# Query projection in fp32r halves, rotated scores in two row halves of the array, the mask added by VectorE, and all cache pages issued by one queue

## What is computed

```python
cq = rms_norm(h @ w_dq)                               # N x 512
q = (cq @ w_uq).reshape(T, 8 heads, 128 + 64)         # 128 plain, 64 to be rotated
q_nope, q_rope = q[..., :128], rope(q[..., 128:], pos)
s = (q_lat . kv_lat + q_rope . kv_rope) * scale       # masked causally, softmax
o_lat = softmax(s) @ kv_lat;  y = (o_lat @ w_uv) @ w_o
```

## Time and profile before

| | |
|---|---|
| median of 3 runs | 3227.74 us |
| the profiled execution | 3235.13 us |
| its span (first to last instruction) | 3233.5 us |
| TensorE busy | 2474.1 us (77%) |
| VectorE busy | 1346.7 us (42%) |
| ScalarE busy | 1083.1 us (33%) |
| granted TensorE clock, mean | 0.866 |

### The profile page before, as it was taken

One profiled execution on the slowest core, in us unless ns is written; L12 is line 12 of the kernel. 1 busy time (PEld: TensorE's weight loads), 2 busy tenths in 40 slices (PEclk: granted clock), 3 DMA queues, 4 the chain that ended last, 5 costly groups with the idle time before them and its releaser, 6 DMA issues. The chain is left out here.

```text
span 3233.5 us, 39140 instructions
## 1 busy us (share of the span) xinstructions
PE 2474.1 (77%) x11571; PEld 1799.5 (56%) x11571; DVE 1346.7 (42%) x2113; ACT 1083.1 (33%) x1738; POOL 405.0 (13%) x492
## 2 busy tenths in 40 slices
PE   3999975858608999896788999997668438999960
PEld 1866654647507777775454666663257326777740
DVE  2311114546534644642771222231145526644647
ACT  1211212331114655653332333231122026655542
POOL 0000001520020010000321000002400020000005
PEclk6899985778759999998798999998778669999985
DMA  6166624630126756664314000006640038755754
GB/s 221 49 239 218 211 96 115 201 113 26 40 104 221 285 208 249 244 223 162 139 64 153 12 23 11 14 9 213 205 147 33 27 119 326 261 212 214 256 208 142
DMA packets 197663, 486.22 MB, mean 150 GB/s; under 512 B 23539, under 2 KB 59604, under 8 KB 191078
## 3 DMA queue, kind: packets, MB, share of 16 engines
q1 hardware_dynamic: 165366, 385.33, 34.3%
q0 software_dynamic: 25152, 74.12, 7.0%
q10 hardware_dynamic: 7056, 25.69, 1.9%
HBM read 423.89 MB, written 64.37 MB: 151 GB/s over the span
## 5 line engine op out<-in xcount | busy, mean ns | idle before, releaser
L1809 DVE TENSOR_TENSOR e_wl<-e_raw,e_wh 128x1024 fp32r<-128x1024 f32 x384 | 447.1, 1220 | 339.7 <-ACT e_wh L1757 332.5
L1757 ACT CAST e_wh<-e_raw 128x1024 fp32r<-128x1024 f32 x384 | 373.8, 1046 | 176.7 <-SPq L1664 74.4
L1716 PE MATMUL e_psG<-e_wh,e_xh 128*128 128x512 f32 x784 | 311.9, 398 | 30.8 <-DVE e_xl L1822 30.8
L1717 PE MATMUL e_psG<-e_wl,e_xh 128*128 128x512 f32 x784 | 311.4, 397 | 0.0
L1718 PE MATMUL e_psG<-e_wh,e_xl 128*128 128x512 f32 x784 | 311.2, 397 | 0.0
L1716 PE MATMUL e_psY<-e_wh,e_hh 128*128 128x512 f32 x392 | 168.2, 429 | 39.4 <-DVE e_hl L1831 39.4
L1716 PEld LDWEIGHTS e_psG<-e_wh,e_xh 128*128 128x128 f32 x784 | 148.2, 189 | 67.4 <-issue 31.6
L309 PE MATMUL in_ps<-in_w_upper,in_h_upper 128*128 128x512 f32 (+1 forms) x432 | 178.7, 414 | 0.0
L310 PE MATMUL in_ps<-in_w_lower,in_h_upper 128*128 128x512 f32 (+1 forms) x432 | 172.7, 400 | 0.0
L311 PE MATMUL in_ps<-in_w_upper,in_h_lower 128*128 128x512 f32 (+1 forms) x432 | 172.0, 398 | 0.0
L1717 PEld LDWEIGHTS e_psG<-e_wl,e_xh 128*128 128x128 f32 x784 | 148.2, 189 | 35.8
(11 more groups left out here) (435 smaller groups left out, 4384.0 us busy)
## 6 DMA issues: line engine op xcount, KB each, us to landing
e_raw<-in_e_gate SPq DMA_DIRECT2D x32, 2048.0 KB
e_raw<-in_e_up SPq DMA_DIRECT2D x32, 2048.0 KB
e_raw<-in_e_down SPq DMA_DIRECT2D x32, 2048.0 KB, 14.8
x<-in_ada_w SPq DMA_DIRECT2D x40, 1024.0 KB, 5.3
yrows<-e_y ACTq DMA_DIRECT2D x49, 512.0 KB, 7.2
x<-in_cache SPq DMA_DIRECT2D x80, 192.0 KB, 3.5
in_w_raw<-in_a_w_in POOLq DMA_DIRECT2D x48, 256.0 KB, 4.4
qkvo<-in_out SPq DMA_DIRECT2D x48, 256.0 KB, 2.3
```

Of the source, the lines that this page charges most:

```text
L1716: T.matmul(out, upper[:, k, :], wh[:, z, cols], start=first and i == 0, stop=False)
L1717: T.matmul(out, upper[:, k, :], wl[:, z, cols], start=False, stop=False)
L1757: S.copy(wh[:, z, c * PC:(c + 1) * PC], raw[:, z, c * PC:(c + 1) * PC]).then_inc(s_hi[z], 1)
L1809: V.tensor_tensor(wl[:, z, at], raw[:, z, at], wh[:, z, at].bitcast(F32), ALU.subtract).then_inc(s_lo[z], 1)
```

## The change

**Latents.** `cqT` is kept as an fp32r upper half `cqh` (ScalarE's copy in `back`) and an fp32r rest `cql`, which VectorE subtracts (`lower(t)`, one more 128 x 512 instruction per tile, after `normalise` of the next tile); TensorE waits for it before it reuses the PSUM tile. The weights `wkv` and `wdq` are placed where `mixT1` will be, which frees memory.

**Query projection.** The head's `wq` is split by ScalarE (`split(h)`, 128 x 1024, to fp32r) and VectorE (`lower(h)`, 128 x 1024). For head h+1 both stand in block i = 2 of head h's loop. TensorE makes three fp32r matmuls where one fp32 matmul stood, over runs of 364, 364 and 360 columns.

**Rotation.** VectorE's product goes to `prod`; ScalarE copies it with its two 64-partition halves swapped (`swap_halves`, two copies of 64 partitions), VectorE adds the two (`add_halves`) into `qr`, so both halves of `qr` hold the rotated query.

**Scores.** Block i above 0 is cut in two column halves w = 64(i+1), each in a PSUM bank of its own. The plain part is one fp32 matmul per half. The rotated part is one fp32 matmul per half with a contraction over 64 partitions, column half 0 on partitions 0 to 63 and half 1 on 64 to 127. The mask product is gone; VectorE adds the mask to the diagonal 128 x 128 in PSUM ahead of the maximum.

**Pages.** POOL issues none. In the heads stage SP issues the same 32 key pages and no values are loaded there. In the sample stage SP issues key units 4 to 15 and value units 0 to 15 (224 pages) in order of use; the values have four buffers. After the last head's projections SP loads head 0's weights once more, for the split that the loop's last pass makes.

The diff, cut to its core:

```diff
@@ stage_combine_latents
-                S.copy(g.cqT[:, :, t * P:t * P + n], psC[:, :, 0:n])
+                S.copy(g.cqh[:, :, t * P:t * P + n], psC[:, :, 0:n])
+            def lower(t):
+                v.wait_ge(s_out, t + 1)
+                V.tensor_tensor(g.cql[:, :, t * P:t * P + n], psC[:, :, 0:n],
+                                g.cqh[:, :, t * P:t * P + n].bitcast(F32), ALU.subtract).then_inc(s_cql, 1)
@@ stage_heads
-        RUNS = ((0, HALF), (HALF, HALF), (SEQ, NSAMP))
+        RUNS = ((0, 364), (364, 364), (728, 360))
-        @block.gpsimd
-            po.dma_start(pt[:], g.page_table).then_inc(s_pt, 16)
-            po.wait_ge(s_pt, 16)
-            for u in range(len(g.vals)):
-                load_unit(po, g, pt, u, g.vals[u], VALUE_COLS, g.s_vals[u])
+            sp.dma_start(pt[:], g.page_table).then_inc(s_pt, 16)
...
+            sp.wait_ge(s_job, JOBS * H + JOBS)
+            weights(0)
@@ tensor
                 pe.wait_ge(s_w, 64 * h + 64)
+                pe.wait_ge(s_wl, h + 1)
-                            mm = T.matmul(psJ[:, z, 0:n], wq[:, k, z * P:(z + 1) * P], g.cqT[:, k, lo:lo + n],
-                                          start=(k == 0), stop=(k == 3))
+                            T.matmul(out, wqh[:, k, cols], g.cqh[:, k, c], start=(k == 0), stop=False)
+                            T.matmul(out, wqh[:, k, cols], g.cql[:, k, c], start=False, stop=False)
+                            mm = T.matmul(out, wql[:, k, cols], g.cqh[:, k, c], start=False, stop=(k == 3))
...
-                        T.matmul(psS[:, par, lo:hi], qn[:, q], kT[:, lo:hi], start=True, stop=False)
-                        mm = T.matmul(psS[:, par, lo:hi], qr[:, q], g.krT[:, lo:hi], start=False, stop=not last)
-                            mm = T.matmul(psS[:, par, i * P:width], g.ident[:], g.qmask[:], start=False, stop=True)
+                    for a in range(parts):
+                        T.matmul(psS[:, par, a, 0:w], qn[:, q], kT[:, a * w:(a + 1) * w], start=True, stop=False)
+                    for a in range(parts):
+                        mm = T.matmul(psS[:, par, a, 0:w], qr[64 * a:64 * a + 64, q],
+                                      g.krT[64 * a:64 * a + 64, a * w:(a + 1) * w], start=False, stop=True)
@@ scalar
+            def split(h):
+                act.wait_ge(s_w, 64 * h + 64)
+                S.copy(wqh[:], wq[:]).then_inc(s_wh, 1)
+            split(0)
...
+                    for a in range(2):
+                        S.copy(swap[64 * a:64 * a + 64, r % 2, 0:n], prod[64 - 64 * a:128 - 64 * a, r % 2, 0:n])
...
                     if i >= 1:
                         output(i - 1)
+                    if i == 2:
+                        split(h + 1)
@@ vector
+            def lower(h):
+                v.wait_ge(s_wh, h + 1)
+                V.tensor_tensor(wql[:], wq[:], wqh[:].bitcast(F32), ALU.subtract).then_inc(s_wl, 1)
...
+                    own = psS[:, par, parts - 1, w - P:w]
+                    V.tensor_tensor(own, own, g.qmask[:], ALU.add)
+                    v.drain()
...
                     if i + 1 < PT:
                         maximum(i + 1)
+                    if i == 2:
+                        lower(h + 1)
@@ stage_sample
+            load_keys(4)
+            for u in range(RV):
+                load_values(u)
+            sp.dma_start(wv, g.w_uv.rearrange("h p n -> p h n")).then_inc(s_wv, 16)
+            for u in range(5, 10):
+                load_keys(u)
+            for u in range(10, UNITS):
+                load_keys(u)
+                load_values(u - 6)
+            for u in range(UNITS - 6, UNITS):
+                load_values(u)
         @block.gpsimd
-            for u in range(len(g.vals), UNITS):
-                if u >= RV:
-                    po.wait_ge(s_vu, u - RV + 1)
-                load_unit(po, g, pt, u, vals[u % RV], VALUE_COLS, s_vals[u % RV])
```

More of the change, by code:

```diff
@@ L2091, in turn_latents @@
                     pe.wait_ge(s_out, t)
+                    pe.wait_ge(s_cql, t)
                 for k in range(4):
@@ L2264, in _ @@
                 normalise(t)
+                if t >= 1:
+                    lower(t - 1)
+            lower(TILES - 1)
 def stage_heads(nc, g):
@@ L2293, in stage_heads @@
         block = ctx.enter_context(nc.Block())
-        RUNS = ((0, HALF), (HALF, HALF), (SEQ, NSAMP))
+        RUNS = ((0, 364), (364, 364), (728, 360))
+        WIDE = 364
+        SAMPLE = slice(SEQ - RUNS[2][0], N - RUNS[2][0])
+        prod, swap = sb("rope_products", [P, 2, WIDE]), sb("rope_swapped", [P, 2, WIDE])
+        s_wh, s_wl, s_swap, s_qr = (sem(x) for x in ("wq_upper", "wq_lower", "halves_swapped", "q_rope_ready"))
         JOBS = 11
         ACT_JOBS = 8 + PT
-        @block.gpsimd
-        def _(po):
-            po.dma_start(pt[:], g.page_table).then_inc(s_pt, 16)
-            po.wait_ge(s_pt, 16)
-            for u in range(len(g.vals)):
-                load_unit(po, g, pt, u, g.vals[u], VALUE_COLS, g.s_vals[u])
         @block.sync
@@ L2417, in _ @@
                     S.copy(qn[:, lo:lo + n], psJ[:, 0, 0:n]).then_inc(s_ja, 1)
+                    if r >= 1:
+                        swap_halves(r - 1)
                 for c in range(2):
@@ L2467, in _, with rotate, add_halves @@
             v.wait_ge(s_c, 16)
+            def lower(h):
+                v.wait_ge(s_wh, h + 1)
+                V.tensor_tensor(wql[:], wq[:], wqh[:].bitcast(F32), ALU.subtract).then_inc(s_wl, 1)
+            lower(0)
             with v.Fori(0, H) as h:
-                for r, (lo, n) in enumerate(RUNS):
+                def rotate(r):
+                    lo, n = RUNS[r]
                     v.wait_ge(s_job, JOBS * h + JOBS + 2 * r + 2)
-                    V.tensor_tensor(qr[:, lo:lo + n], psJ[:, 1, 0:n], trig[:, lo:lo + n], ALU.mult).then_inc(s_jv, 1)
+                    V.tensor_tensor(prod[:, r % 2, 0:n], psJ[:, 1, 0:n], trig[:, lo:lo + n], ALU.mult).then_inc(s_jv, 1)
+                def add_halves(r):
+                    lo, n = RUNS[r]
+                    v.wait_ge(s_swap, 3 * h + r + 1)
+                    V.tensor_tensor(qr[:, lo:lo + n], prod[:, r % 2, 0:n], swap[:, r % 2, 0:n], ALU.add).then_inc(s_qr, 1)
+                rotate(0)
+                rotate(1)
+                add_halves(0)
+                v.drain()
+                rotate(2)
+                add_halves(1)
+                add_halves(2)
                 def maximum(i):
@@ L2557, in _, with load_keys @@
             sp.wait_ge(s_pt, 16)
-            for u in range(len(g.keys), UNITS):
+            def load_keys(u):
                 if u >= RK:
@@ L2562, in _, with load_values @@
                 load_unit(sp, g, pt, u, keys[u % RK], KEY_COLS, s_keys[u % RK])
-                if u == len(g.keys):
-                    sp.dma_start(wv, g.w_uv.rearrange("h p n -> p h n")).then_inc(s_wv, 16)
+            def load_values(u):
+                if u >= RV:
+                    sp.wait_ge(s_vu, u - RV + 1)
+                load_unit(sp, g, pt, u, vals[u % RV], VALUE_COLS, s_vals[u % RV])
+            load_keys(4)
[9 more added lines that the diff above has]
+                load_values(u)
         @block.gpsimd
```

66 lines of the change are left out of this document (43 added, 23 removed).

## The result

The changed kernel takes **3341.58 us** (median; 3337.87 to 3344.08) against 3227.44 for the one before (3225.49 to 3228.67): a ratio of 1.0353, 95% interval 1.0335 to 1.0371. It is slower, by 114 us between the medians. The two profiled executions lie closer, 3235.13 before and 3337.87 after, 102.7 apart, and it is this difference that the traces can share out. I cut both at SP's first issue of a stage: 6.1 less up to the latents stage (code that the change leaves alone), 0.4 more in the latents stage, **3.5 more in the heads** (1718.54 to 2191.87 before, 1712.79 to 2189.66 after), **102.4 more in the sample stage** (to 2361.05 and 2461.19), 2.6 more behind it.

A forecast was written before the change was run, and what follows sets the result against it. It took page issue on the queues to bound the sample stage and TensorE the heads. Sample +104, heads -7, clock +8, once +5.5 made +110.5, rounded to +111: 3346 profiled, less 7.4 gives median 3339, range 3308 to 3364.

The forecast's parts named there:

- A page's time is the queue's: Page loads: the interval is the cost of issuing, above all the page-number read, whatever the size; 1.09 to 1.14 us.
- The rival that bytes set it: Sample stage: value pages cost two thirds, 0.75 us, so sample +57 and total 3292; chance 0.08.
- Sample stage +104: SP issues 224 pages at 1.12 us without stopping; last page issued at about 2446 instead of 2341.75.
- Issuing is nearly free: Sample stage rival: one queue gives bytes as fast as two, below 0.63 us a page; 3214, faster; chance 0.03.
- Projection -3.8 a head: Heads, query projection: three fp32r matmuls per former fp32 one take 11.9 us a head instead of 15.72.
- Row halves -3.75 and mode changes +3.4: Heads, rotated scores: 64-row halves run side by side, but two mode changes in each of 8 blocks cost 0.21 each.
- Mask -1.7, its waits +1.4: Heads: dropping eight 0.22 us mask products saves TensorE 1.7; VectorE's addition lengthens waits in four blocks by 1.4.
- The chain's 0.37: Heads: VectorE's mask addition ahead of the maximum, 0.29 us plus some 0.08 until the next instruction.
- Split and lower +3.6: Heads: VectorE's lower waits for ScalarE's split ahead of block 3's division, delaying TensorE 3.6 us a head.
- Clock +8: Heads: extra idling makes the other five heads lose 1.6 us each at lower clock; between nothing and +15.
- Once +5.5: One-time costs: head 0's uncovered split and lower +3.7, its split for head 1 about +1, last latents lower +0.8.
- -7 and -17 below, +5 and +25 above: Forecast spread: page interval gives -7 to +5, heads -17 to +25, stated as 3312 to 3365.

The follow-up runs named there:

- fixed_pages: The changed kernel with page numbers written into the program instead of read from the table, so other pages are loaded; sample stage 127.2 us, kernel 3175.2 us.
- after: The changed kernel itself, against the kernel before the change: 3341.6 us, ratio 1.0353.
- two_queues: The changed kernel with POOL issuing the sample stage's value pages again and SP keys alone; sample stage 181.7 us, kernel 3249.7 us, ratio to the kernel before 1.0065.
- full_rows: The changed kernel with the rotated scores over all 128 rows again, without swap copies and additions; heads 491.3 us, kernel 3345.4 us.
- mask_pe: The changed kernel with the causal mask back as a TensorE product and no VectorE addition; heads 470.5 us, kernel 3329.1 us.
- late_split: The changed kernel with the next head's weights split later, ScalarE after block 6 and VectorE after block 7; heads 449.9 us, kernel 3306.6 us.
- late_mask: The changed kernel with the next head's weights split later and the mask back on TensorE; heads 439.3 us, kernel 3305.8 us.
- queue_only: The kernel before with SP also issuing the sample stage's value pages, five buffers and early loads kept; sample stage 246.3 us, kernel 3308.7 us, ratio 1.0237.

## Why the prediction was right

It said 3339.0 (3308 to 3364), slower; measured 3341.6. The profiled execution was to be 3346 and took 3337.9. How near that is, is partly luck. The forecast was 111 us for the profiled execution, less 7.4 for the median; the profiled executions came out 102.7 apart and the medians 114. The stages ahead of the latents, which the change leaves alone, were 6.1 us shorter in the profiled execution, and between kernels that share all code ahead of the heads the start of the heads varies by 13 us. No term of the sum stands for that. What is shown is the main term. By the steps:

- **A page's time is the queue's.** Right, and now shown: 1.11 for 128 KB, 1.09 for 192 KB, 0.51 without the lookup. "The read of the page number above all" was half right: of 1.11 us the read is 0.33 and the comparisons with it 0.28, the transfer itself 0.50. One reading of the rows was loose: while both queues issue, also has slices of 323 and 374 GB/s, above the 305 that it names. The rival that bytes set it would have left fixed_pages at 270 and is out.
- **Sample stage +104.** Measured +102.4; SP never stopped, and the stage's tail was as before.
- **Issuing is nearly free** (the rival on the other side): false for this loop, since it needed a page under 0.63. Its 127 us for the bytes was right: fixed_pages takes 127.2. The rule of the Trainium skill ("DMA: Bandwidth & Descriptors", section "Issuing engines are not separate DMA queues"), that several issuers save only sequencer time, usually small, holds in its first half: that time is all that two queues save here. It is not small, 90 us between after and two_queues.
- **Projection -3.8 a head.** TensorE starts it at 2131.26 and is through at 2143.33: 12.07 for 15.72, -3.65.
- **Row halves -3.75 and mode changes +3.4.** Order right, the term for the changes mis-sized: 0.29 for two in block 7 instead of 0.42, so 2.3 a head by that block, which would make the net -1.4. By full_rows it is about -1 a head, not -0.35. The 0.21 each from the mLSTM rounds was an upper bound.
- **Mask -1.7, its waits +1.4.** The sign of the net is wrong: +0.8 a head (mask_pe), +1.3 with the late split. The chain's 0.37 was right (addition 0.30 and 0.08 behind it). What failed is that I credited the product's 0.22 in all eight blocks: in a block where TensorE then waits, taking work off it gains nothing, and the wait grows by the product's time as well as by the addition.
- **Split and lower +3.6.** 3.4 to 4.0 at block 3 of every head; late_split gives 3.4 back.
- **Clock +8.** Each head of after loses 0.40 + 0.65 + 0.68 = 1.7 us behind the stall (the three records of late_split against its own), 13.8 in all. Before, three heads lost 1.6 each, 4.8. So +9: right. That a version without the stall gets it back was wrong (late_split's expectation).
- **Once +5.5.** The first projection waits 11.7 where it waited 9.7 before, and the latents stage grew 0.4; under half of what I took. The 3.7 for head 0 had some 0.9 in it ("pages close behind") that no row gives.

The heads as a whole were to grow by 5.7 (-7, +8 and 4.7 of the once) and grew by 3.5. In TensorE's busy time the parts measured are -29.2 for the projection, -8 for the halves, -12.5 for the mask and +9 for the clock, -41 where the stage shows -39.4; so the decomposition closes within 2 us. But the halves gave 5 more and the mask cost 9 more than I had put, and these misses cancel in the sum: that it is close is no proof of its terms. The 2.6 us behind the sample stage and the 6.1 less ahead of the latents I did not foresee, and they are unexplained. The spread that the prediction works out, 3312 to 3365, does not follow from its terms either: -7 and -17 below, +5 and +25 above, give 3315 to 3369; 3341.6 lies well inside both.

## What to carry to other kernels

A transfer whose address is read from a table costs its queue a read, its comparisons and its issue, one after another; count instructions per page on each queue before moving pages between queues, and share the pages until the bytes are the limit. Work taken off an engine pays only in the stretches where the engine does not go on to wait, and an addition on the chain it waits for pays in none. A helper for the next round (here the split of the next head's weights) belongs where its engine is idle at the end of a round, not ahead of an instruction that another engine needs.

## What the runs showed that I had not expected

- Reading four page numbers with one call brings a page from 1.11 to 0.87 us on SP and from 1.15 to 0.92 on POOL, and eight ahead of their transfers, still two calls, bring no more. The comparisons of each page stay.
- The two comparisons with the smallest and largest page cost nearly as much as a read, 0.28 us a page, a quarter of the interval: without them the sample stage is 64.9 us shorter (271.5 to 206.6).
- The two waits of a head do not by themselves tell where TensorE falls to the low clock. In after all eight heads fell behind the 3.5 us stall (granted clock 0.60 over 4.3 us in the head shown, so mostly 1.2 GHz) and none behind the 2.2 us wait at the end. Without the stall all eight fell behind that wait in late_split (0.72 for 6.1 us in the one shown), four of eight in late_mask, where it is 2.0 us, and three of eight before, where it is 2.1. In full_rows three heads fell at both places, in mask_pe two at neither. What decides it is open.
- The stages ahead of the heads ended anywhere between 1702.0 and 1715.3 us in the twelve kernels that have the same code there (after and all but queue_only), nearly as much apart as full_rows moved the heads. The cause is open.
